# Dense projections of a hybrid encoder: three split float32r matmuls replaced by one float32 matmul

## The chip, the cores and the metric

One core of one Trainium2 chip runs the whole kernel. The metric is the device time of one execution in microseconds, the median of several runs.

## What is computed

A two-layer encoder trunk on 256 tokens of width 1024, all in float32. Layer 0 mixes tokens with a bidirectional diagonal state-space mixer, layer 1 with neighbourhood attention. Each is followed by a mixture of 32 experts (two of them for each token) and a gated embedding. The parts that matter here:

```python
def _rmsnorm(x, g):
    y = x * lax.rsqrt(jnp.mean(x * x, axis=-1, keepdims=True) + RMS_EPS)
    return y * g

for i in range(2):
    h = _rmsnorm(x, norm_mix[i])
    x = x + (_s5_mixer(h, ...) if i == 0 else _nat_mixer(h, nat_w_qkv[0], ...))   # qkv = h @ w_qkv, 1024 x 3072
    h = _rmsnorm(x, norm_ffn[i])
    x = x + _hier_moe(h, ...)
    gate = jax.nn.sigmoid(_rmsnorm(x, norm_ple[i]) @ ple_w_gate[i])               # 1024 x 1024
    x = x + gate * (p[i] @ ple_w_proj[i])
```

In the attention, q and k are normalised per head (64 values), and a score bias of relative positions is added.

## The kernel before

Every engine has its own program, written out by hand in order, with semaphores between them. The order in time is: state-space layer, MoE block 0, embedding gate 0 (`ple(0)`), qkv projection, attention with its output product, MoE block 1, embedding gate 1 (`ple(1)`), store.

**Weights.** SyncE's queue loads every weight in an order fixed in the program into a ring of six slots in SBUF. A slot's next load waits on the semaphore that says that its last content is used up; for the gate and qkv weights this is `split_done`. The gate weight of 1024 x 1024 comes as two halves of 512 columns (`ga`, `gb`), the qkv weight as six parts of 512 columns (0 and 1 are q, 2 and 3 are k, 4 and 5 are v), each 2 MB and each in one slot. `IT["ple"]` and `IT["qkv"]` hold their item numbers. A part has four chunks of two 128-row blocks; `place` numbers the chunks in the order in which TensorE takes them.

**Transposed x.** A norm's input x is kept in four pieces (128 tokens x 512 columns). For each, TensorE makes four transposes into a PSUM bank (`piece_T`, line 1714). For the dense products ScalarE copies the bank, rounded to float32r, into `hTh` (`piece_evict`, line 781), and VectorE then writes the remainder into `hTl` (`split_lo`, line 1141). The norm's per-token factor `rstd` is applied at the end, when the products are evicted; the norm's per-column gain goes into the weights.

**Weights' split.** For each 128-row block of 512 columns, ScalarE multiplies the loaded weights by the gain and rounds them to float32r into `dwh`, a ring of four chunks (`dense_hi`, line 814); VectorE writes the remainder in place of the loaded weights (`dense_lo`, line 1151). ScalarE waits for the DMA (`arrived`) and for `dwh` to come free.

**Product.** `dense_mm` (line 1741) makes, for each block and for each of the two token tiles, three float32r matmuls: high x by low weights, low x by high weights, high by high, all into one PSUM bank:

```python
for w, (a_, b_) in enumerate(((hTh, lo), (hTl, hi), (hTh, hi))):
    ins = mm(PS[:, b, :], a_[:, 2 * c + k, r], b_, ...)
```

**Order.** In `ple(i)` TensorE transposes four pieces of x, takes the four chunks of `ga`, three of `gb`, (for i = 0) the transposes of the first two pieces of the next norm, and the last chunk of `gb`. Those pieces are ready when `ple_gate` (ScalarE, sigmoid) and `ple_evict` (VectorE, product and sum) of the first columns are done. Then come qkv parts 0 and 1, interleaved by halves with the transposes of the last two pieces, and parts 2 to 5 in turn, into two pairs of PSUM banks. Each part is evicted by ScalarE (tokens 0 to 127) and VectorE (128 to 255) in `qkv_evict`; parts 0 to 3 go on through `square` (ScalarE), `sums` (VectorE), a power on GpSimd (`qk_pow`, line 728), `qk_norm` (VectorE), transposes on TensorE (`qk_T`, line 2146) and `q_evict` or `k_evict`. GpSimd issues the loads of the score bias (`bias_load`, line 743) in the same queue, one group before each power. TensorE's `qk_T` groups stand after chunk 2 of part 3, chunks 0 and 2 of part 4 and chunk 1 of part 5; the first block of `scores` stands after chunk 2 of part 5.

Elsewhere the kernel uses plain float32 matmuls on loaded weights: the state-space output product (line 1906), the experts (lines 1951 and 1977), the embedding projection (`proj`, line 2009) and the attention output product (line 2209).

Of the kernel before, what the change touches and what calls it, by code (L numbers as in the profile page):

```python
# [72 lines left out]
def program(nc, I, out):  # L73
    ctx = ExitStack()
    with ctx:
# [146 lines left out]
        for i in range(2):  # L222
            done.update({moe_item[i] + e: ("gu_done", NP * i + e // 2 + 1) for e in range(NE)})

            done.update({n: ("split_done", place[n if (n, 3) in place else IT["ple"][i][0], 3] + 1)
                         for n in IT["ple"][i]})
        done.update({n: ("split_done", place[n, 3] + 1) for n in IT["qkv"]})
# [31 lines left out]
        gain_of = {n: 2 for n in IT["ple"][0]}  # L259
        gain_of.update({n: 3 for n in IT["qkv"]})  # L260
        gain_of.update({n: 6 for n in IT["ple"][1]})

# [102 lines left out]
        hTh = at("hTh", [P, KD, T], F32R, A_XG)  # L365
        hTl = at("hTl", [P, KD, T], F32R, A_XG + 8192)
        dwh = at("dwh", [P, 4, 2, 512], F32R, A_XG + 16384)
        ringr = [at(f"ringr{s}", [P, KD, 512], F32R, A_R + s * RS * 4) for s in range(4)]
        SPLIT = {2: 0, 3: 1, 5: 2}

        def dense_w(n, c):

            s = items[n][0]
            return (ring[s][:, 1024 * c:1024 * c + 1024].rearrange("p (k n) -> p k n", k=2),
                    ringr[s][:, 2 * c:2 * c + 2, :])
# [61 lines left out]
        def _(sp):  # L437
# [105 lines left out]
            for i in range(2):  # L543
                if i:
                    for w, e in ((4, 0), (5, 1)):
                        sp.wait_ge(S("split_done"), place[IT["qkv"][w], 3] + 1)
                        load_gate(i, e)
                        load_up(i, e)
                        load_down(i, e)
# [212 lines left out]
        def _(ac):  # L762
# [14 lines left out]
            def piece_evict(n, m):  # L777
                c, t = divmod(m, 2)
                ac.wait_ge(S("x_T"), pieces(n) + m + 1)
                if n in SPLIT:  # L780
                    ac.activation(hTh[:, 4 * c:4 * c + 4, P * t:P * t + P],
                                  PS[:, 4 + 2 * t + c, :].rearrange("p (k t) -> p k t", k=4), ACT.Copy)\
                        .then_inc(S("hTh_ready"), 1)
                else:
                    ac.activation(hT[:, 4 * c:4 * c + 4, P * t:P * t + P],
                                  PS[:, 2 + t, :].rearrange("p (k t) -> p k t", k=4), ACT.Copy)\
                        .then_inc(S("hT_ready"), 1)
# [16 lines left out]

            def dense_hi(n, c):

                m = place[n, c]
                if c == 0:
                    arrived(ac, n)
                if m >= 4:  # L810
                    ac.wait_ge(S("split_done"), m - 3)
                for k in range(2):
                    g = 2 * c + k
                    ins = ac.activation(dwh[:, m % 4, k], dense_w(n, c)[0][:, k, :], ACT.Copy,  # L814
                                        scale=gcol[:, gain_of[n], g:g + 1])
                ins.then_inc(S("dense_hi"), 1)
# [145 lines left out]
            def moe(i):  # L962
# [24 lines left out]
                for c in range(4):  # L987
                    dense_hi(IT["ple"][i][0], c)
# [8 lines left out]
            def ple_gate(i, n):  # L997
                k = 4 * i + n
                c, t = divmod(n, 2)
                ac.wait_ge(S("split_done"), place[IT["ple"][i][2 * c], 3] + 1)  # L1000
# [6 lines left out]
            def ple(i):  # L1007
                n = 2 + 3 * i
                for m in range(4):
                    piece_evict(n, m)  # L1010
                for m in range(4):
                    piece_sq(n, m)
                gb = IT["ple"][i][2]
                for c in range(3):
                    dense_hi(gb, c)
                ple_gate(i, 0)
                ple_gate(i, 1)
                dense_hi(gb, 3)
                if i == 0:
                    q0, q1 = IT["qkv"][0:2]  # L1020
                    dense_hi(q0, 0)
                    dense_hi(q0, 1)
                    piece_evict(3, 0)
                    piece_evict(3, 1)
                    dense_hi(q1, 0)
                    piece_sq(3, 0)
                    piece_sq(3, 1)
                ple_gate(i, 2)
                ple_gate(i, 3)
                if i == 0:  # L1030
                    dense_hi(q1, 1)
                    dense_hi(q0, 2)
                    piece_evict(3, 2)
                    piece_evict(3, 3)
                    dense_hi(q0, 3)
                    piece_sq(3, 2)
                    piece_sq(3, 3)
                    dense_hi(q1, 2)
                    dense_hi(q1, 3)
# [5 lines left out]
            def qkv_evict(w):  # L1045
                ac.wait_ge(S("split_done"), place[IT["qkv"][w], 3] + 1)
# [23 lines left out]
            for w in range(2, 6):  # L1070
                for c in range(4):
                    dense_hi(IT["qkv"][w], c)
                    if (w, c) == (2, 1):
                        qkv_evict(0)
                        square(0)
                    if (w, c) == (4, 1):
                        q_evict(0)
                    if (w, c) == (4, 3):
                        q_evict(1)
                qkv_evict(w - 1)  # L1080
                if w < 5:
                    square(w - 1)
# [29 lines left out]
        def _(ve):  # L1112
# [24 lines left out]
            def split_lo(n, m):  # L1137
                c, t = divmod(m, 2)
                ve.wait_ge(S("hTh_ready"), 4 * SPLIT[n] + m + 1)
                r = hTh[:, 4 * c:4 * c + 4, P * t:P * t + P]  # L1140
                tt(hTl[:, 4 * c:4 * c + 4, P * t:P * t + P], PS[:, 4 + 2 * t + c, :].rearrange("p (k t) -> p k t", k=4),  # L1141
                   r.bitcast(F32), ALU.subtract).then_inc(S("hTl_ready"), 1)

            def dense_lo(n, c):

                m = place[n, c]
                ve.wait_ge(S("dense_hi"), m + 1)
                w, lo = dense_w(n, c)
                for k in range(2):
                    g = 2 * c + k  # L1150
                    ins = stt(lo[:, k, :], w[:, k, :], gcol[:, gain_of[n], g:g + 1], dwh[:, m % 4, k].bitcast(F32),  # L1151
                              ALU.mult, ALU.subtract)
                ins.then_inc(S("dense_lo"), 1)
# [401 lines left out]
            def ple(i):  # L1555
                ga, _, gb = IT["ple"][i]
                dense_lo(ga, 0)
                dense_lo(ga, 1)
                for m in range(4):
                    split_lo(2 + 3 * i, m)  # L1560
                dense_lo(ga, 2)
                dense_lo(ga, 3)
                stats(2 + 3 * i)
                for c in range(3):
                    dense_lo(gb, c)
                ple_evict(i, 0)
                ple_evict(i, 1)
                dense_lo(gb, 3)
                if i == 0:
                    q0, q1 = IT["qkv"][0:2]  # L1570
                    dense_lo(q0, 0)
                    dense_lo(q0, 1)
                    split_lo(3, 0)
                    split_lo(3, 1)
                    dense_lo(q1, 0)
                ple_evict(i, 2)
                ple_evict(i, 3)
                if i == 0:
                    dense_lo(q1, 1)
                    dense_lo(q0, 2)  # L1580
                    split_lo(3, 2)
                    split_lo(3, 3)
                    dense_lo(q0, 3)
                    stats(3)
                    dense_lo(q1, 2)
                    dense_lo(q1, 3)
# [5 lines left out]
            def qkv_evict(w):  # L1592
                ve.wait_ge(S("split_done"), place[IT["qkv"][w], 3] + 1)
# [25 lines left out]
            for w in range(2, 6):  # L1619
                for c in range(4):  # L1620
                    dense_lo(IT["qkv"][w], c)
                    if (w, c) == (2, 1):
                        qkv_evict(0)
                        sums(0)
                    if c == 1 and w > 2:
                        qk_norm(w - 2)
                    if (w, c) == (5, 1):
                        k_evict(2)
                if w == 2:
                    qk_norm(0)  # L1630
                qkv_evict(w - 1)
                if w < 5:
                    sums(w - 1)
# [54 lines left out]
        def _(pe):  # L1688
# [13 lines left out]
            def piece_T(n, m):  # L1702
# [3 lines left out]
                if n in SPLIT:  # L1706
# [25 lines left out]
            def dense_mm(n, c, b0, b1):  # L1732

                m = place[n, c]
# [367 lines left out]
            def ple(i):  # L2102
# [7 lines left out]
                for c in range(4):  # L2110
                    if c % 2 == 0:
                        pe.wait_ge(S("hTl_ready"), 4 * SPLIT[norm] + 2 + c)
# [13 lines left out]
            pe.wait_ge(S("hTl_ready"), 4 * SPLIT[3] + 2)  # L2126
# [6 lines left out]
            pe.wait_ge(S("hTl_ready"), 4 * SPLIT[3] + 4)  # L2133
# [131 lines left out]
```

## Time and profile before

| | |
|---|---|
| median of 3 runs | 796.95 us (794.77 to 798.34) |
| the profiled execution | 796.67 us, of which the span of its instructions is 794.9 us |
| TensorE matmul busy | 738.1 us, 93% of the span |
| VectorE, ScalarE, GpSimd busy | 409.2, 277.9, 111.2 us |
| granted TensorE clock, mean | 0.987 of full speed |
| DMA | 247.33 MB, mean 311 GB/s |

Busy time says how long an engine had an instruction under way, not that it was needed then; the chain that ended last says which work set the end. Matmuls overlap in the pipeline, so their mean duration is longer than their distance. The two dense stages lie at 384 to 478 us and at 766 to 789 us of the span.

### The profile page before, as it was taken

What the parts mean: (1) busy time and instruction counts of PE and PEld (TensorE: products, weight loads), DVE (VectorE), ACT (ScalarE), POOL (GpSimd) and SP (SyncE); (2) the same over time, 40 slices, a digit from 0 to 9 for tenths busy, and PEclk for the clock granted to TensorE, in tenths of its full rate; (3) what the DMA queues carried; (4) which work ended last, traced back from release to release, by engine and by line L of the source; (5) the groups of instructions that cost most, each with busy time, mean ns of one, the idle gap of its engine ahead of it and who ended that gap; (6) DMA issues with size and microseconds to landing.
All of it is one profiled execution on the core that took longest, in us unless ns stands there. A gap on an engine that the chain in (4) does not pass through costs nothing.

```text
span 794.9 us, 12786 instructions
## 1 busy us (share of the span) xinstructions
PE 738.1 (93%) x5121; PEld 470.4 (59%) x5121; DVE 409.2 (51%) x913; ACT 277.9 (35%) x521; POOL 111.2 (14%) x112
## 2 busy tenths in 40 slices
PE   4877789799999999989999998999999999999896
PEld 3755655465655555544788884555655555564465
DVE  6998833644343343432786868345443343434174
ACT  6351144252221222213675746425121222222163
POOL 5697320000000000000206621000000000000000
PEclk9989999999999999999999999999999999999999
DMA  8157693659999999999657789843999999999921
GB/s 274 42 142 222 172 356 127 264 206 423 420 421 420 420 421 421 421 420 397 220 206 236 215 265 327 337 196 113 421 421 420 421 421 421 421 419 421 406 95 53
DMA packets 64244, 247.33 MB, mean 311 GB/s; under 512 B 22244, under 2 KB 23832, under 8 KB 39224
## 3 DMA queue, kind: packets, MB, share of 16 engines
q1 hardware_dynamic: 62152, 243.14, 78.3%
q0 software_dynamic: 2032, 3.35, 1.9%
q8 instruction: 42, 0.69, 0.3%
q14 instruction: 18, 0.15, 0.1%
HBM read 242.85 MB, written 3.06 MB: 309 GB/s over the span
## 4 chain that ended last, share of the span: by engine, by line
PE 68%; DMA 10%; DVE 10%; SPq 5%; POOL 4%; issue 1%; ACT 1%; DVEq 0%
PE PS L1951 21%; PE PS L1741 14%; PE PS L1977 11%; DMA ring<-in_moe_w_down 6%; PE PS L1987 5%; PE PS L2209 4%; DMA ring<-in_moe_w_up 3%; PE PS L1906 3%; POOL s5V L680 2%; PE PS L1921 2%; PE PS L2009 2%; POOL s5W L680 2%; SPq L471 2%; SPq L455 1%; PE PS L1839 1%
## 5 line engine op out<-in xcount | busy, mean ns | idle before, releaser
L1951 PE MATMUL PS<-ring,xw 128*64 128x256 f32 x2016 | 227.7, 379 | 6.8 <-DMA ring<-in_moe_w_up 3.0
L1951 PEld LDWEIGHTS PS<-ring,xw 128*64 128x64 f32 x2016 | 149.5, 137 | 88.8 <-issue 17.5
L1977 PE MATMUL PS<-ring,actT 128*64 128x512 f32 x512 | 116.9, 598 | 2.4 <-DMA ring<-in_moe_w_down 1.3
L1442 DVE COPY actT<-PS 128x256 f32<-128x256 f32 x32 | 13.6, 424 | 159.7 <-PE PS L1960 159.7
L959 ACT ACTIVATE ohi<-PS 128x512 fp32r<-128x512 f32 x64 | 38.2, 597 | 145.8 <-PE PS L1977 145.8
L1456 DVE TENSOR_TENSOR olo<-PS,ohi 128x512 fp32r<-128x512 f32 x64 | 44.3, 692 | 83.3 <-ACT ohi L959 83.2
L652 POOL TENSOR_TENSOR rstd<-ms,mhalf 128x2 f32<-128x2 f32 x6 | 4.2, 706 | 589.8 <-DVE ms L1126 583.4
L1977 PEld LDWEIGHTS PS<-ring,actT 128*64 128x64 f32 x512 | 34.3, 136 | 67.9 <-issue 66.2
L951 ACT ACTIVATE act<-PS,wslot 128x256 f32<-128x256 f32 x32 | 15.2, 476 | 164.9 <-PE PS L1951 164.9
L1425 DVE SCALAR_TENSOR_TENSOR act<-rows,pid 128x256 f32<-128x256 f32 x128 | 61.9, 483 | 14.0 <-DMA rows<-rows_d 10.6
L1741 PE MATMUL PS<-ringr,hTh 128*128 128x512 f32 x160 | 63.2, 395 | 1.4 <-DVE hTl L1141 1.4
L1741 PE MATMUL PS<-dwh,hTh 128*128 128x512 f32 x160 | 62.4, 390 | 0.0
L1741 PE MATMUL PS<-dwh,hTl 128*128 128x512 f32 x160 | 62.3, 389 | 0.0
L1151 DVE SCALAR_TENSOR_TENSOR ringr<-ring,gcol,dwh 128x512 fp32r<-128x512 f32 x80 | 55.3, 746 | 12.0 <-ACT dwh L814 12.0
L814 ACT ACTIVATE dwh<-ring,gcol 128x512 fp32r<-128x512 f32 x80 | 52.2, 714 | 15.7 <-PE PS L1741 13.3
L1987 PE MATMUL PS<-ohi,selT 128*128 128x512 f32 x128 | 53.9, 421 | 0.2
L1987 PE MATMUL PS<-olo,selT 128*128 128x512 f32 x128 | 50.4, 394 | 0.0
L945 ACT ACTIVATE xw<-xg 128x512 f32 x60 | 38.1, 636 | 3.1 <-issue 2.4
L1741 PEld LDWEIGHTS PS<-ringr,hTh 128*128 128x128 f32 x160 | 30.0, 188 | 8.0 <-DVE hTl L1141 1.9
L1741 PEld LDWEIGHTS PS<-dwh,hTh 128*128 128x128 f32 x160 | 30.0, 188 | 6.4
L1741 PEld LDWEIGHTS PS<-dwh,hTl 128*128 128x128 f32 x160 | 30.1, 188 | 5.9
L2209 PE MATMUL PS<-ring,oT 128*128 128x512 f32 x64 | 30.1, 605 | 0.0
(326 smaller groups left out, 960.4 us busy)
## 6 DMA issues: line engine op xcount, KB each, us to landing
ring<-in_moe_w_down SPq DMA_DIRECT2D x64, 1024.0 KB, 20.8
ring<-in_moe_w_up SPq DMA_DIRECT2D x64, 1024.0 KB, 18.8
ring<-in_moe_w_gate SPq DMA_DIRECT2D x62, 1024.0 KB, 16.5
ring<-in_nat_w_qkv SPq DMA_DIRECT2D x6, 2048.0 KB
ring<-in_ple_w_gate SPq DMA_DIRECT2D x4, 2048.0 KB
ring<-in_s_w_out SPq DMA_DIRECT2D x2, 2048.0 KB
ring<-in_nat_w_o SPq DMA_DIRECT2D x2, 2048.0 KB
ring<-in_s_w_in SPq DMA_DIRECT2D x1, 2048.0 KB
```

Source lines behind the costliest of these rows:

```text
L680: pool.tensor_tensor(dst, dst, tmp[n % 2][:, :, :, :], ALU.subtract if minus else ALU.add)\
L814: ins = ac.activation(dwh[:, m % 4, k], dense_w(n, c)[0][:, k, :], ACT.Copy, scale=gcol[:, gain_of[n], g:g + 1])
L945: ac.activation(xw[:, p % 2, :, CAP * h_:CAP * h_ + CAP], xg[:, :, bass.ds(f, CAP)], ACT.Copy)\
L959: ac.activation(ohi[:, 512 * n:512 * n + 512], PS[:, 2 + n, :], ACT.Copy)\
L1151: ins = stt(lo[:, k, :], w[:, k, :], gcol[:, gain_of[n], g:g + 1], dwh[:, m % 4, k].bitcast(F32), ALU.mult, ALU.subtract)
L1425: link(stt(act[:, p % 2].rearrange("p k f -> p (k f)"), slotrow[:, n % 2, :], pid[:, p:p + 1], row, ALU.is_equal, ALU.mult, accum_out=wpar ...
L1456: tt(olo[:, cs], PS[:, 2 + n, :], ohi[:, cs].bitcast(F32), ALU.subtract)\
L1741: ins = mm(PS[:, b, :], a_[:, 2 * c + k, r], b_, start=(c, k, w) == (0, 0, 0), stop=(c, k, w) == (3, 1, 2))
L1951: ins = mm(PS[CAP * h_:CAP * h_ + CAP, 0, FF * u:FF * u + FF], xw[:, p % 2, k, CAP * h_:CAP * h_ + CAP], wv[h_][:, FF * k:FF * k + FF], st ...
L1977: ins = mm(PS[CAP * h_:CAP * h_ + CAP, 2 + n, :], actT[:, k, CAP * h_:CAP * h_ + CAP], wd[h_][:, k, 512 * n:512 * n + 512], start=k == 0, ...
L1987: ins = mm(PS[:, 4 + 2 * t + n, :], selT[p % 2][:, P * t:P * t + P], o_half[:, 512 * n:512 * n + 512], start=(p, w) == (0, 0), stop=(p, w) ...
L2209: ins = mm(PS[:, 4 + 2 * c + t, :], oT[:, k, P * t:P * t + P], wv[:, k, :], start=k == 0, stop=k == KD - 1)
```

## The change

The products of gates and qkv become one float32 matmul for each block and token tile, directly on the loaded weights. The gain is multiplied into the transposed x as VectorE evicts it from PSUM (`hT_gain`, into `hTg`, float32). `dense_hi`, `dense_lo`, `split_lo`, `dwh` and ScalarE's part of `piece_evict` for these norms go. TensorE waits for each part's DMA itself. The semaphore `split_done` is now `dense_done`. The order of TensorE's work stays; in the qkv part, the loops of ScalarE and VectorE are written anew without the splits.

```diff
-                if n in SPLIT:
-                    ac.activation(hTh[:, 4 * c:4 * c + 4, P * t:P * t + P],
-                                  PS[:, 4 + 2 * t + c, :].rearrange("p (k t) -> p k t", k=4), ACT.Copy)\
-                        .then_inc(S("hTh_ready"), 1)
...
-            def dense_hi(n, c):
...
-                    ins = ac.activation(dwh[:, m % 4, k], dense_w(n, c)[0][:, k, :], ACT.Copy,
-                                        scale=gcol[:, gain_of[n], g:g + 1])
...
@@ ScalarE, qkv
-            for w in range(2, 6):
-                for c in range(4):
-                    dense_hi(IT["qkv"][w], c)
...
+            for w in range(5):
+                qkv_evict(w)
+                if w < 4:
+                    square(w)
+                if w in (2, 3):
+                    q_evict(w - 2)
@@ VectorE
-            def split_lo(n, m):
+            def hT_gain(n, m):
+
                 c, t = divmod(m, 2)
...
+                ve.wait_ge(S("x_T"), pieces(n) + m + 1)
+                tt(hTg[:, 4 * c:4 * c + 4, P * t:P * t + P], PS[:, 4 + 2 * t + c, :].rearrange("p (k t) -> p k t", k=4),
+                   bc(gcol[:, BLOCK_GAIN[n], 4 * c:4 * c + 4], 2, P), ALU.mult).then_inc(S("hTg_ready"), 1)
...
-                    ins = stt(lo[:, k, :], w[:, k, :], gcol[:, gain_of[n], g:g + 1], dwh[:, m % 4, k].bitcast(F32),
-                              ALU.mult, ALU.subtract)
...
@@ VectorE, qkv
+            for w in range(4):
+                qkv_evict(w)
+                if w:
+                    qk_norm(w - 1)
+                sums(w)
+            k_evict(2)
+            qk_norm(3)
+            qkv_evict(4)
             k_evict(3)
@@ TensorE, dense_mm
-                m = place[n, c]
-                pe.wait_ge(S("dense_lo"), m + 1)
+                if c == 0:
+                    arrived(pe, n)
                 for k in range(2):
                     for t, b in enumerate((b0, b1)):
-                        r = slice(P * t, P * t + P)
-                        hi, lo = dwh[:, m % 4, k, :], dense_w(n, c)[1][:, k, :]
-                        for w, (a_, b_) in enumerate(((hTh, lo), (hTl, hi), (hTh, hi))):
-                            ins = mm(PS[:, b, :], a_[:, 2 * c + k, r], b_, start=(c, k, w) == (0, 0, 0),
-                                     stop=(c, k, w) == (3, 1, 2))
-                ins.then_inc(S("split_done"), 1)
+                        ins = mm(PS[:, b, :], hTg[:, 2 * c + k, P * t:P * t + P], dense_w(n, c)[:, k, :],
+                                 start=(c, k) == (0, 0), stop=(c, k) == (3, 1))
+                ins.then_inc(S("dense_done"), 1)
```

## Rows read from the trace of the kernel before

**Rows 1.** The page, part 2: tenths of busy or granted clock, and GB/s.

```profile
PEclk9989999999999999999999999999999999999999
GB/s 274 42 142 222 172 356 127 264 206 423 420 421 420 420 421 421 421 420 397 220 206 236 215 265 327 337 196 113 421 421 420 421 421 421 421 419 421 406 95 53
```

**Rows 2.** The chain that ended last, in order of time: start us, us, what.

```profile
113.50 10.30 PE PS L1906 x24
...
382.83 1.30 DVE hTl L1141 x2
384.17 19.34 PE PS L1741 x84
403.51 0.88 PE PS L1714 x8
...
413.44 35.41 PE PS L1741 x156
...
455.18 0.87 PE PS L2146 x8
...
517.27 3.44 PE PS L2209 x8
...
766.56 22.09 PE PS L1741 x96
```

**Rows 3.** Groups by line and shape: count, busy us, mean ns, idle before.

```profile
L1741 PE MATMUL PS<-ringr,hTh 128*128 128x512 f32 x160 | 63.2, 395 | 1.4 <-DVE hTl L1141 1.4
...
L1151 DVE SCALAR_TENSOR_TENSOR ringr<-ring,gcol,dwh 128x512 fp32r<-128x512 f32 x80 | 55.3, 746 | 12.0 <-ACT dwh L814 12.0
...
L814 ACT ACTIVATE dwh<-ring,gcol 128x512 fp32r<-128x512 f32 x80 | 52.2, 714 | 15.7 <-PE PS L1741 13.3 <-DMA ring<-in_ple_w_gate 2.2
...
L1247 DVE TENSOR_TENSOR s5T<-PS,mask 128x512 f32<-128x512 f32 x8 | 5.4, 681 | 2.6 <-POOL s5V L680 2.4
```

**Rows 4.** Timelines of ScalarE, TensorE and VectorE before the first dense stage.

```profile
374.52 5.01 ACT L814 ACTIVATE dwh<-ring,gcol 128x512 fp32r<-128x512 f32 x8 [1.06 <-DMA ring<-in_ple_w_gate]
...
381.56 1.91 PE L1714 MATMUL PS<-ident,x 128*128 128x128 f32 x16
...
382.20 2.06 ACT L781 ACTIVATE hTh<-PS 128x512 fp32r<-128x512 f32 x4 [2.67 <-PE PS L1714]
...
382.83 2.48 DVE L1141 TENSOR_TENSOR hTl<-PS,hTh 128x512 fp32r<-128x512 f32 x4 [0.29 <-ACT hTh L781]
```

**Rows 5.** ScalarE's timeline in gate 0, where the first half's products end.

```profile
394.02 1.28 ACT L1004 ACT_TABLE_LOAD   x1
395.38 1.27 ACT L1004 ACTIVATE sg<-PS,rstd 128x512 f32<-128x512 f32 x2
```

**Rows 6.** GpSimd's timeline during qkv: bias loads and one power.

```profile
419.96 4.79 POOL L743 DMA_DIRECT2D bias<-bias_d  x8
...
452.45 4.81 POOL L743 DMA_DIRECT2D bias<-bias_d  x8
460.14 3.35 POOL L728 TENSOR_TENSOR qrs<-qms,mhalf 128x16 f32<-128x16 f32 x1 [2.88 <-DVE qms L1604]
```

**Rows 7.** VectorE's timeline during qkv: one reduction and one multiplication.

```profile
458.63 1.22 DVE L1603 TENSOR_REDUCE qss<-sq 128x16 f32<-128x1024 f32 x1 [1.57 <-ACT sq L1059]
...
463.52 1.22 DVE L1609 TENSOR_TENSOR qk<-qk,qrs 128x1024 f32<-128x1024 f32 x1 [0.82 <-POOL qrs L728]
```

**Rows 8.** SyncE's timeline, DMA issues (us to landing), and windows (the last number is GB/s).

```profile
395.37 0.40 SPq L449 DMA_DIRECT2D ring<-in_nat_w_qkv  x1
...
bias<-bias_d POOLq DMA_DIRECT2D x4, 72.0 KB, 6.8
...
390.00:392.00 2.00, 2.00 (x10) 1.66 (x9) 0.75 (x3) 1.28 (x2) 2.00 (x4) 1.00 0.24 14
...
404.00:406.00 2.00, 2.00 (x12) 1.71 (x11) 1.29 (x2) 2.00 (x4) 0.00 (x0) 1.00 0.00 0
...
762.00:764.00 2.00, 2.00 (x6) 0.76 (x5) 2.00 (x4) 0.00 (x0) 0.00 (x0) 1.00 0.00 0
```

More of the change, by code:

```diff
@@ L223, in program @@
             done.update({moe_item[i] + e: ("gu_done", NP * i + e // 2 + 1) for e in range(NE)})
-            done.update({n: ("split_done", place[n if (n, 3) in place else IT["ple"][i][0], 3] + 1)
+            done.update({n: ("dense_done", place[n if (n, 3) in place else IT["ple"][i][0], 3] + 1)
                          for n in IT["ple"][i]})
-        done.update({n: ("split_done", place[n, 3] + 1) for n in IT["qkv"]})
+        done.update({n: ("dense_done", place[n, 3] + 1) for n in IT["qkv"]})
         done.update({n: ("wo_done", 2 * c + 2) for c, n in enumerate(IT["wo"])})
@@ L258, in program @@
         ROW_GAIN = {1: 1, 4: 5}
-        gain_of = {n: 2 for n in IT["ple"][0]}
-        gain_of.update({n: 3 for n in IT["qkv"]})
-        gain_of.update({n: 6 for n in IT["ple"][1]})
         def pieces(n):
@@ L363, in program @@
         rr = at("rr", [P, 4, 2 * TT], F32, A_W + 1184)
[L365 to L369, printed above, removed]
+        hTg = at("hTg", [P, KD, T], F32, A_XG)
+        DENSE = {2: 0, 3: 1, 5: 2}
         def dense_w(n, c):
             s = items[n][0]
-            return (ring[s][:, 1024 * c:1024 * c + 1024].rearrange("p (k n) -> p k n", k=2),
-                    ringr[s][:, 2 * c:2 * c + 2, :])
+            return ring[s][:, 1024 * c:1024 * c + 1024].rearrange("p (k n) -> p k n", k=2)
         pT = at("pT", [P, 2, T], F32, A_H + 8192)
@@ L545, in _ @@
                     for w, e in ((4, 0), (5, 1)):
-                        sp.wait_ge(S("split_done"), place[IT["qkv"][w], 3] + 1)
+                        sp.wait_ge(S("dense_done"), place[IT["qkv"][w], 3] + 1)
                         load_gate(i, e)
@@ L779, in piece_evict @@
                 ac.wait_ge(S("x_T"), pieces(n) + m + 1)
-                if n in SPLIT:
-                    ac.activation(hTh[:, 4 * c:4 * c + 4, P * t:P * t + P],
-                                  PS[:, 4 + 2 * t + c, :].rearrange("p (k t) -> p k t", k=4), ACT.Copy)\
-                        .then_inc(S("hTh_ready"), 1)
[L784 to L787, printed above, removed]
+                ac.activation(hT[:, 4 * c:4 * c + 4, P * t:P * t + P],
+                              PS[:, 2 + t, :].rearrange("p (k t) -> p k t", k=4), ACT.Copy)\
+                    .then_inc(S("hT_ready"), 1)
             def piece_hi(n, m):
@@ L803, in front @@
                     piece_hi(n, m)
-            def dense_hi(n, c):
-                m = place[n, c]
[L808 to L813, printed above, removed]
-                    ins = ac.activation(dwh[:, m % 4, k], dense_w(n, c)[0][:, k, :], ACT.Copy,
-                                        scale=gcol[:, gain_of[n], g:g + 1])
-                ins.then_inc(S("dense_hi"), 1)
             def norm_evict(dst, t):
@@ L986, in moe @@
                 out_hi(i, NP - 1)
-                for c in range(4):
-                    dense_hi(IT["ple"][i][0], c)
                 def more(n):
@@ L999, in ple_gate @@
                 c, t = divmod(n, 2)
-                ac.wait_ge(S("split_done"), place[IT["ple"][i][2 * c], 3] + 1)
+                ac.wait_ge(S("dense_done"), place[IT["ple"][i][2 * c], 3] + 1)
                 ac.wait_ge(S("rstd_ready"), 3 + 3 * i)
@@ L1009, in ple @@
                 for m in range(4):
-                    piece_evict(n, m)
-                for m in range(4):
                     piece_sq(n, m)
-                gb = IT["ple"][i][2]
-                for c in range(3):
-                    dense_hi(gb, c)
                 ple_gate(i, 0)
                 ple_gate(i, 1)
-                dense_hi(gb, 3)
                 if i == 0:
[L1020 to L1025, printed above, removed]
                     piece_sq(3, 0)
@@ L1030, in ple @@
                 if i == 0:
[L1031 to L1035, printed above, removed]
                     piece_sq(3, 2)
                     piece_sq(3, 3)
-                    dense_hi(q1, 2)
-                    dense_hi(q1, 3)
             moe(0)
@@ L1045, in qkv_evict @@
             def qkv_evict(w):
-                ac.wait_ge(S("split_done"), place[IT["qkv"][w], 3] + 1)
+                ac.wait_ge(S("dense_done"), place[IT["qkv"][w], 3] + 1)
                 if w == 0:
@@ L1069, in _ @@
             link(ac.activation(qkw8[:, :], qkw[:, 0:1], ACT.Copy, scale=1 / math.sqrt(HD)))
-            for w in range(2, 6):
-                for c in range(4):
-                    dense_hi(IT["qkv"][w], c)
[L1073 to L1082, printed above, removed]
+            for w in range(5):
[4 more added lines that the diff above has]
+                    q_evict(w - 2)
             ac.activation(warm[:, :], ones[:, 0:1], ACT.Exp)
@@ L1135, in piece_lo @@
                    hhi[:, t, :, 64 * c:64 * c + 64].bitcast(F32), ALU.subtract).then_inc(S("hlo_ready"), 1)
-            def split_lo(n, m):
+            def hT_gain(n, m):
                 c, t = divmod(m, 2)
[L1139 to L1150, printed above, removed]
-                    ins = stt(lo[:, k, :], w[:, k, :], gcol[:, gain_of[n], g:g + 1], dwh[:, m % 4, k].bitcast(F32),
-                              ALU.mult, ALU.subtract)
-                ins.then_inc(S("dense_lo"), 1)
+                ve.wait_ge(S("x_T"), pieces(n) + m + 1)
+                tt(hTg[:, 4 * c:4 * c + 4, P * t:P * t + P], PS[:, 4 + 2 * t + c, :].rearrange("p (k t) -> p k t", k=4),
+                   bc(gcol[:, BLOCK_GAIN[n], 4 * c:4 * c + 4], 2, P), ALU.mult).then_inc(S("hTg_ready"), 1)
             ve.wait_ge(S("lam_loaded"), 48)
@@ L1555, in ple @@
             def ple(i):
-                ga, _, gb = IT["ple"][i]
-                dense_lo(ga, 0)
-                dense_lo(ga, 1)
                 for m in range(4):
-                    split_lo(2 + 3 * i, m)
-                dense_lo(ga, 2)
-                dense_lo(ga, 3)
+                    hT_gain(2 + 3 * i, m)
                 stats(2 + 3 * i)
-                for c in range(3):
-                    dense_lo(gb, c)
                 ple_evict(i, 0)
                 ple_evict(i, 1)
-                dense_lo(gb, 3)
                 if i == 0:
[L1570 to L1575, printed above, removed]
+                    hT_gain(3, 0)
+                    hT_gain(3, 1)
                 ple_evict(i, 2)
@@ L1578, in ple @@
                 if i == 0:
[L1579 to L1583, printed above, removed]
+                    hT_gain(3, 2)
+                    hT_gain(3, 3)
                     stats(3)
-                    dense_lo(q1, 2)
-                    dense_lo(q1, 3)
             moe(0)
@@ L1592, in qkv_evict @@
             def qkv_evict(w):
-                ve.wait_ge(S("split_done"), place[IT["qkv"][w], 3] + 1)
+                ve.wait_ge(S("dense_done"), place[IT["qkv"][w], 3] + 1)
                 if w == 0:
@@ L1618, in _ @@
             ve.wait_ge(S("qkw_loaded"), 64)
[L1619 to L1633, printed above, removed]
+            for w in range(4):
[6 more added lines that the diff above has]
+            qkv_evict(4)
             k_evict(3)
@@ L1705, in piece_T @@
                 pe.wait_ge(S("x_piece"), pieces(n) + m + 1)
-                if n in SPLIT:
+                if n in DENSE:
                     b = 4 + 2 * t + c
@@ L2111, in ple @@
                     if c % 2 == 0:
-                        pe.wait_ge(S("hTl_ready"), 4 * SPLIT[norm] + 2 + c)
+                        pe.wait_ge(S("hTg_ready"), 4 * DENSE[norm] + 2 + c)
                     dense_mm(ga, c, 4, 6)
@@ L2125, in _ @@
             q0, q1 = IT["qkv"][0:2]
-            pe.wait_ge(S("hTl_ready"), 4 * SPLIT[3] + 2)
+            pe.wait_ge(S("hTg_ready"), 4 * DENSE[3] + 2)
             dense_mm(q0, 0, 0, 1)
@@ L2132, in _ @@
             dense_mm(q1, 1, 2, 3)
-            pe.wait_ge(S("hTl_ready"), 4 * SPLIT[3] + 4)
+            pe.wait_ge(S("hTg_ready"), 4 * DENSE[3] + 4)
             dense_mm(q0, 2, 0, 1)
```

1 line of the change is left out of this document (removed).

## The prediction

> **What bounds the kernel now.** I read the chain that ended last first, in order of time, then the instruction groups, then the timelines of each engine around the two dense stages, and last the DMA windows. The kernel has four regimes: the state-space layer, two MoE blocks, and between and behind them the projections that the change rewrites. The MoE blocks run with the load queue full: the GB/s row holds 420 in slices 10 to 18 and 29 to 38 [rows 1], and the change touches nothing in them. In the dense stages the load queue is far from full (206 to 265 GB/s in slices 20 to 24), and the chain is TensorE alone: the split matmuls of line 1741, broken only by transposes and by one score block [rows 2]. So work taken from TensorE there counts in full, and work taken from VectorE and ScalarE counts only where it stands on the chain.
>
> There are 160 products of one 128-row block of weights with one token tile, each made of three float32r matmuls; the group row has 160 of the first kind, and the other two kinds have as many, 480 in all [rows 3]. A group's mean duration (395 ns) overlaps its neighbours, so I take the pace from the chain: 19.34 us for 84, 35.41 for 156, 22.09 for 96, that is 0.230, 0.227 and 0.230 us each [rows 2]. The first dense stage holds 384 of them (eight pieces of the chain, 87.8 us in all), the second 96 (22.1 us). Together 109.9 us.
>
> **The change, part by part.**
>
> *Plain float32 matmuls.* 480 go, 160 come: 128 in the first stage (16 for each of two gate halves and six qkv parts), 32 in the second. Their shape, 128 x 128 stationary and 128 x 512 float32 moving from the ring, is in this kernel already: 24 in 10.30 us on line 1906 and 8 in 3.44 us on line 2209 [rows 2], 0.429 and 0.430 us each, back to back, with a new stationary tile each. At 0.430 the first stage needs 55.0 us, the second 13.8. Gain: 87.8 - 55.0 = 32.8 and 22.1 - 13.8 = 8.3, together 41.1 us. The bounds of this term are narrow: 0.427 to 0.435 us give 160 x 0.003 = 0.5 more or 0.8 less.
>
> The Trainium skill, "FP8 and Floating Point Precision", section "TensorE Precision Notes", says the opposite of these rows: true float32 takes four passes through the array, and only the reduced form one. By this rule the change would lose time. The rows have the float32 matmul at 1.9 times the float32r one, not four, so the sum goes by them and the rule is a rival below.
>
> *The splits of weights.* 80 ScalarE copies of 714 ns and 80 VectorE operations of 746 ns go [rows 3]. None is on the chain of the first stage; they ran beside TensorE, so they count nothing by themselves. What they hid: TensorE now waits for the weights' own loads. In the first stage the first half's weights were being read at 374.52 [rows 4], nine microseconds before use, and by 390 the DMA had fallen to 14 GB/s [rows 8]: both gate halves and the first two qkv parts had landed by then, and at the new pace they are wanted at 383.5, 390.4, 398.1 and 402.4. A later part was issued at 395.37 and traffic was zero at 404 [rows 8]: under 9 us from issue to landing. At the new pace part 2 is issued when the first gate half is done (390.4) and wanted at 412.9, part 3 issued 398.1, wanted 419.8, parts 4 and 5 issued 409.4 and 412.9, wanted 427.5 and 436.1. The least distance between issue and want is 18 us, twice a load's nine. In the second stage traffic is zero at 762 [rows 8], and the second half is wanted at about 772.8. So I cost the loads at nothing.
>
> *Norm's scale put into transposed x.* ScalarE's rounding copy and VectorE's subtraction, one after the other, become one VectorE multiplication for each piece. Its price is not shown; the nearest is a PSUM by broadcast multiply of the same 128 x 512, 681 ns [rows 3], and I take 0.69. Were the broadcast inside the row to double it, 0.7 us would be added to the start of each stage; that end stays in the range. Now: transposes from 381.56 over 1.91 us, ScalarE at 382.20, VectorE from 382.83 at 0.62 a piece, TensorE at 384.17 after two pieces [rows 2, 4]. After: VectorE starts at 382.2, two pieces are done by about 383.5, when the transposes end too. Gain 0.65 us, in both stages: 1.3 us.
>
> *Sigmoid and the next norm.* ScalarE's table load (394.02, 1.28 us [rows 5]) stood behind a split and just fitted in; without splits ScalarE is idle from about 382 and loads it early. With gate half 0 done at 390.4, two sigmoids of 0.7 and four VectorE steps of 0.69 put the first two pieces of x ready at 392.8 and 394.2; TensorE wants to transpose them after three quarters of the second half, at 395.5: 1.3 us to spare. The other two pieces: half 1 done 398.1, ready 400.6 and 402.0; TensorE comes at 401.6 and at 402.0. I count 0.4 us of stall here.
>
> *The q and k norm.* This is what runs late next, and it is the only narrow place. VectorE's mean squares go to GpSimd, which takes 3.35 us for the power and stands, in its own queue, behind bias loads of 4.8 us (the first and the last of four; the two between issue four DMAs, not eight, so half of that) [rows 6]; VectorE's reduction and multiplication are 1.22 us each [rows 7]. Followed step by step at the new pace: GpSimd issues the first bias loads until about 412, takes the powers at 412.8, 418.8 and 424.9, issues the last bias loads 428.3 to 433.1, takes the last power until 436.5, and VectorE multiplies until 437.7. TensorE wants the last transposes of k at 439.5. Slack 1.8 us. The loads of the bias must land before VectorE's first score at 442.7; 6.8 us from issue [rows 8] makes 439.9. Behind the reordered VectorE queue stand the eviction of v's first half and k's last eviction, 438.4 and 442.0; the scores that need them come at 442.1 and 444.4. All hidden, by little.
>
> *What follows.* With its six groups of transposes (5.2 us) and the first score block (0.6) the stage ends, with the second scores, 33.1 us earlier than now. Attention, its output product, the router and the second MoE block are released by TensorE's own progress and shift as a whole; the prefetch of the first experts starts at the last two qkv parts, keeping its distance to the MoE block. The tail behind the last dense matmul (788.65 to 794.9: sigmoid, product, sum, store) stays as it is.
>
> Sum: 41.1 + 1.3 - 0.4 = 42.0 us. The profiled execution took 796.67 us (span 794.9, 1.8 around it), 0.3 under the median 796.95. So 796.67 - 42.0 = 754.7, and for a median 755.
>
> **Rivals.**
>
> *Four passes.* If a float32 matmul of these operands took four times a pass of 0.228 us, 160 x 0.912 = 145.9 us would stand against 109.9: 36 us more, less 1.3 at the starts: 831 us, slower than before. It decides from 0.69 us a matmul on. Against it: three lines of the kernel at 0.43, of the same shape, in full stream. 2%. By the skill's figure of four passes at 2.4 GHz (an estimate from "FP8 and Floating Point Precision", 0.853 us) it would be about 822; no row here shows such a matmul.
>
> *GpSimd's chain becomes the bound.* If its bias issues or powers slip, each microsecond beyond 1.8 goes to TensorE. One or two issue blocks of 4.8 us too many, less the slack of 1.8, give 3.0 to 7.8 us: 758 to 763. For it: 3.35 us powers in strict order behind DMA issues. Against it: the steps are from rows and still leave slack. 13%.
>
> *The loads are the bound.* With the stage a third shorter the same bytes (six parts, two output parts and the first experts) need a higher rate. If weights arrived only at the 220 GB/s that the stage shows now, eight loads of 2.1 MB would take 76 us instead of 62: 14 us lost, 769. Against it: the stage is at 390 to 410 GB/s whenever a load is under way, and zero between; the 220 is demand. 4%.
>
> *The gain is lost in MoE's load-bound stretch.* If the second MoE block started short of experts, it would end by its loads, and the first stage's 33 us could shrink to 20 (768). Against it: prefetch and MoE start shift together. 2%.
>
> *TensorE's clock.* The PEclk row is at 9 or more in all slices but one [rows 1], and the stage leaves no new gap in TensorE's work; left out as a case of its own.
>
> **How the numbers follow.** Likeliest, 79%: all terms as costed, 755 us, own range 752.5 to 757.5 (matmul pace, multiply price, stalls of 0 to 2 us, a median that wanders by 0.2 to 0.3%). GpSimd's chain 13% (758 to 763), loads 4%, MoE 2%, four passes 2%. The range for 8 in 10, drawn towards the GpSimd case's middle: 752 to 760. A measurement of this kernel can tell about 0.5%, 4 us. All cases but four passes are faster by far more: faster 0.97, same 0.01, slower 0.02.
>
> **What the profile after should show.** 160 matmuls on the dense line at 0.43 us pace, in place of 480; the first stage some 61 us long instead of 94; ScalarE busy about 58 us less (52.2 of the splits, three groups of copies of 2.06) and VectorE about 55 us less; a first dense matmul about 1.3 us after ScalarE used to start copying; PE idle in the stage under 1 us, and where any, before the transposes of x's last pieces or of k's last ones, released by VectorE; granted clock 1.00; DMA above 300 GB/s there; MoE's length unchanged to 0.5 us. The prediction is wrong if the matmul's pace differs from 0.43, if waits on the ring's loads or on k's norm appear on the chain, or if the second MoE block grows.

## The result: 825 us, slower, and where the profile after puts it

The changed kernel takes 825.22 us (median of 4 runs, 822.82 to 826.92) against 797.13 us before: ratio 1.0354, 95% interval 1.0317 to 1.0391. The forecast was 755 us. In the experiments below, two runs fell into a slower state of the chip (835.54 us of kernel half, 1330.24 us of kernel cols) and are left out of the medians. The profiled execution has a span of 824.3 us, 29.4 more than before.

The page of the changed kernel, part 1, and its costliest group of the dense products (line 1649 is the new `dense_mm`):

```profile
PE 765.6 (93%) x4961; PEld 440.4 (53%) x4961; DVE 355.6 (43%) x833; ACT 222.0 (27%) x429; POOL 109.2 (13%) x112
...
L1649 PE MATMUL PS<-ring,hTg 128*128 128x512 f32 x320 | 139.1, 593 | 0.1
...
L2117 PE MATMUL PS<-ring,oT 128*128 128x512 f32 x64 | 30.1, 605 | 0.0
```

VectorE has 53.6 us less to do and ScalarE 55.9 us less, as forecast, and none of it shows in the time. TensorE has 27.5 us more. The count of matmuls says why: the code makes 160 products (four chunks of two blocks for two token tiles in each of ten parts), and the trace has 320 matmuls. One float32 product is two matmul records (entries of the trace), each with its own weight load. The last row says the same of a line that the change left alone: the attention output product is called 2 x 2 x 8 = 32 times and has 64 records, in this trace as in that of before.

The chain that ended last in the changed kernel, in order of time (start us, us, what):

```profile
384.21 1.30 DVE hTg L1087 x2
385.56 24.30 PE PS L1649 x56
409.86 0.87 PE PS L1625 x8
410.73 10.30 PE PS L1649 x24
...
421.90 44.64 PE PS L1649 x104
466.54 0.87 PE PS L2054 x8
...
498.11 3.63 PE PS L1649 x8
...
788.92 1.30 DVE hTg L1087 x2
790.27 27.75 PE PS L1649 x64
```

A record takes 0.429 us (44.64 for 104), as I had read in [rows 2]; a product, being two, takes 0.859. The three float32r matmuls that it replaces took 3 x 0.2285 = 0.685 (0.227 to 0.230 each in the chain of before). The chain is the same as in [rows 2], still TensorE alone, and its sum explains the time:

| term | before | after | difference |
|---|---|---|---|
| dense products, first stage (eight pieces of the chain each) | 87.8 | 110.4 | +22.6 |
| dense products, second stage | 22.1 | 27.8 | +5.7 |
| from the last projection matmul to the first product, two stages | 2 x 2.45 | 2 x 1.82 | -1.3 |
| start of the second half of the first projection, ahead of all changed code | 378.29 | 380.30 | +2.0 |

Together 29.0 of the 29.4 us. The last term is no work of the change: the same point lies anywhere from 377.40 (v3one) to 381.74 (two_qkw) in the profiled executions below, so the first MoE block's end spreads by 4 us. Without it the terms make 27.0 us, and the medians differ by 28.1.

### The profile page after: what moved, and what is told of

The parts are those of the page before. It is cut to its first block, busy times and chain, and to the rows that moved or that the text cites. A ratio compares the mean times of both kernels' runs of the same rounds, so it can differ in the third digit from the quotient of the medians.

```text
span 824.3 us, 12281 instructions
## 1 busy us (share of the span) xinstructions
PE 765.6 (93%) x4961; PEld 440.4 (53%) x4961; DVE 355.6 (43%) x833; ACT 222.0 (27%) x429; POOL 109.2 (13%) x112
## 4 chain that ended last, share of the span: by engine, by line
PE 69%; DVE 10%; SPq 8%; DMA 6%; POOL 4%; issue 1%; ACT 1%; DVEq 0%
PE PS L1859 21%; PE PS L1649 17%; PE PS L1885 10%; DMA ring<-in_moe_w_down 6%; PE PS L1895 5%; PE PS L2117 4%; PE PS L1814 3%; SPq L463 2%; POOL s5V L672 2%; SPq L456 2%; SPq L441 2%; PE PS L1829 2%; SPq L447 2%; PE PS L1917 2%; POOL s5W L672 2%
## 5 line engine op out<-in xcount | busy, mean ns | idle before, releaser
L1649 PE MATMUL PS<-ring,hTg 128*128 128x512 f32 x320 | 139.1, 593 | 0.1
L1649 PEld LDWEIGHTS PS<-ring,hTg 128*128 128x128 f32 x320 | 60.1, 190 | 73.0 <-issue 72.4
L1814 PE MATMUL PS<-ring,yT 128*128 128x512 f32 x64 | 28.4, 593 | 0.0
L1895 PEld LDWEIGHTS PS<-ohi,selT 128*128 128x128 f32 x128 | 24.1, 188 | 5.7 <-DVE olo L1391 1.1
L1895 PEld LDWEIGHTS PS<-olo,selT 128*128 128x128 f32 x128 | 24.1, 189 | 4.6 <-issue 0.5
L1486 DVE TENSOR_TENSOR sg<-sg,PS 128x512 f32<-128x512 f32 x8 | 5.5, 684 | 41.0 <-ACT sg L976 41.0
L1657 PE MATMUL PS<-iota_slot,ident 128*128 128x512 f32 x40 | 21.4, 674 | 0.0
L1774 PE MATMUL PS<-s5V,s5W 64*128 64x128 f32 x256 | 16.2, 277 | 5.1 <-issue 2.2
```

The costliest lines, as they stand in the source:

```text
L1649: ins = mm(PS[:, b, :], hTg[:, 2 * c + k, P * t:P * t + P], dense_w(n, c)[:, k, :], start=(c, k) == (0, 0), stop=(c, k) == (3, 1))
L1657: mm(PS[:, b, :], ident[:, :], iota_slot[:, :], start=True, stop=True)
L1814: ins = mm(PS[:, 4 + 2 * (n % 2) + w, :], yT[4][:, k, P * t:P * t + P], wv[:, k, 512 * c:512 * c + 512], start=k == 0, stop=k == 3)
L1895: ins = mm(PS[:, 4 + 2 * t + n, :], selT[p % 2][:, P * t:P * t + P], o_half[:, 512 * n:512 * n + 512], start=(p, w) == (0, 0), stop=(p, w) ...
```

## Experiments

### The pace that was forecast, with half of each product

```diff
-                for k in range(2):
+                for k in range(1):
```

> The changed kernel with half of each dense product: of the two 128-row blocks of a chunk only the first is multiplied, so the other half of the contraction is left out. 80 float32 products instead of 160; everything else as in the changed kernel. Theory A (a float32 product is two instruction pairs on TensorE, 0.859 us together, and this alone made the kernel slower): 80 x 0.859 = 68.7 us less than the changed kernel's 825.2, so 756.5, within 2 us. This is the TensorE time per chunk (1.72 us) that the prediction had assumed, so it also tests the prediction's other terms. Rival B (the q and k norm with GpSimd's queue, or the weights' loads, would have bound the stage anyway): 759 to 769, with TensorE idle before the transposes of k or before a part. Rival C (the loss is from waits, not from the length of the products): above 790.

Measured: 756.62 us (median of three runs), ratio 0.9471 (0.9426 to 0.9516) against 798.87 us before in the same job. That is theory A's 756.5, and below rival B's 759. The group of line 1649 and the first stage's end in the chain:

```profile
L1649 PE MATMUL PS<-ring,hTg 128*128 128x512 f32 x160 | 70.5, 594 | 0.1
```

```profile
436.18 5.15 PE PS L1649 x12
441.33 0.89 PE PS L2054 x8
...
444.08 10.46 DMA vb<-vt
454.54 0.14 issue
454.68 0.69 PE PS L2099 x16
```

And GpSimd's timeline, bias loads and the last power:

```profile
428.86 4.81 POOL L735 DMA_DIRECT2D bias<-bias_d  x8
433.68 2.93 POOL L720 TENSOR_TENSOR qrs<-qms,mhalf 128x16 f32<-128x16 f32 x1
```

This kernel gives TensorE the length of product that I had assumed for the whole change. It is 42.3 us under before, where I had said 42.0. The stage starts at 385.19, 1.7 us later than I had worked out, by the spread named above. Apart from that, the last bias loads end at 433.7 (forecast 433.1), the last power at 436.6 (436.5), and TensorE comes to the last transposes of k at 441.3 (439.5 + 1.7 = 441.2). Up to there the schedule was right; only the length of a product was not. What I had not seen is the load of v's bands: the four loads of the first bands were issued 442.5 to 444.6, and the larger two took 8.7 us to land, where the same loads take 2.4 in the changed kernel and 4.0 in the one before. The loads of the first two experts were under way beside them (issued from 437.9 and from 446.5 on). The first products of probabilities and values waited 1.1 us for the bands. Nor had I seen what follows the wait, which I had ruled out as a case of its own: the granted clock is 1.00 up to 455 us, with TensorE busy only 0.66 of the 2 us from 452 to 454, then 0.66 from 455 to 456 and 0.50, the lower of its two levels (1.2 of 2.4 GHz), from 456 to 458. The same groups of the chain, first there and then behind it:

```profile
455.36 1.06 PE PS L2075 x16
456.42 1.04 PE PS L2087 x4
...
460.55 0.60 PE PS L2075 x16
461.15 0.59 PE PS L2087 x4
```

With the products of values (1.05 against 0.62) and the first output products (2.03 against 1.91) this is 1.5 us lost. The profiled execution shows it: its span is 37.8 us shorter than before, which is, within 0.1, the 42.0 less the 1.7 us of the later start, the wait of 1.1 and these 1.5. That the medians agree to 0.3 us is partly luck.

### Columns or instructions

```diff
-                        ins = mm(PS[:, b, :], hTg[...], dense_w(n, c)[:, k, :], ...)
+                        for q in (0, 1):
+                            s_ = slice(256 * q, 256 * q + 256)
+                            ins = mm(PS[:, b, s_], hTg[...], dense_w(n, c)[:, k, s_], ...)
```

> The changed kernel with each float32 product of 512 columns issued as two of 256 columns on the same stationary tile: twice the matmuls and weight loads, the same columns streamed. Theory A (the pace is set by streamed columns, 0.43 us for 512 columns in each of two instruction pairs): 640 records of 0.215 us, no change, 825 to 828. Rival D (the pace is set per instruction pair, by the weight load and issue): the 137 us of dense products grow, up to twice as long (962) if nothing depends on the columns.

Measured: 825.83 us (median of three runs), 1.0331 (1.0281 to 1.0381) of before, the changed kernel's time. The groups by shape of this kernel:

```profile
L1651 PE MATMUL PS<-ring,hTg 128*128 128x256 f32 x640 | 139.9, 380 | 0.1
L1651 PEld LDWEIGHTS PS<-ring,hTg 128*128 128x128 f32 x640 | 120.9, 190 | 16.9 <-DVE hTg L1087 0.6 <-issue 0.2
```

320 more weight loads, and the busy time goes from 139.1 to 139.9 us. The columns streamed set the pace, and a record costs what its columns cost, 0.216 us for 256 (44.90 us for 208 in its chain); the weight loads of 190 ns are hidden behind even the halved matmuls. Rival D falls.

### One of the three float32r products less

```diff
-                        for w, (a_, b_) in enumerate(((hTh, lo), (hTl, hi), (hTh, hi))):
+                        for w, (a_, b_) in enumerate(((hTh, lo), (hTh, hi))):
```

> The kernel before with two of the three float32r products: low x by high weights is left out, all splits stay. 320 instead of 480 float32r matmuls at 0.2285 us. Theory A (the dense stages are bound by TensorE's products alone): 36.5 us less than before, 797.1 - 36.5 = 760.6, within 2 us. Rival B (other engines or loads are just behind): the splits of VectorE need 1.42 us a chunk against 1.83 us of products, so only waits on norm, bias or loads could hold it up: 765 to 775.

Measured: 781.23 us, 0.9789 (0.9752 to 0.9826). It is faster than before, by 1.7 to 2.5%, but misses the forecast by 20 us. The chain of this kernel:

```profile
404.73 2.65 DVE ringr L1151 x4
407.38 1.20 DVE hTl L1141 x2
408.58 1.32 DVE ringr L1151 x2
410.26 1.16 POOL rstd L652
411.42 1.58 POOL qkw L719 x3
413.00 5.77 DMA qkw<-in_nat_k_norm
...
420.47 1.19 DVE ringr L1151 x2
```

TensorE's products are off the chain from 389.5 to 463.1 us. VectorE with its splits is on it, and a 1 KB load of the norm's gains, issued late in GpSimd's queue, on which ScalarE waits 7.6 us. In the kernel before, the same wait was 1.36 us and hidden. Theory A as I had put it (the stages are bound by products alone) doesn't hold at this length of product. To see that this was no odd execution, I ran the same kernel once more.

> The two-product kernel of run two once more, for one look: whether the 20 us by which it missed its forecast stand in the same places. Theory E (with less TensorE work, the 7.6 us wait of ScalarE on the load of the q and k norm's gains, and the coupled chain of VectorE's splits, mean squares and GpSimd's power, take over): span 777 to 781, the same wait on that load of about 7 us. Theory F (a single disturbed execution): span near 760.

Measured: 784.11 us in a single run, ScalarE waiting 7.5 us at the same place. The span is 782.4, 1.4 above theory E's range, and the start of the second half of the first projection lies 3.9 us later than in run two (381.74 against 377.82). Theory E stands in the main, F falls.

### The scale in x alone

```diff
+                tt(hTf[...], PS[:, 4 + 2 * t + c, :]..., bc(gcol[:, BLOCK_GAIN[n], 4 * c:4 * c + 4], 2, P), ALU.mult)
...
-                    ins = ac.activation(dwh[:, m % 4, k], w[:, k, :], ACT.Copy, scale=gcol[...])
+                    ins = ac.activation(dwh[:, m % 4, k], w[:, k, :], ACT.Copy)
```

> One part of the change alone: the norm's scale is multiplied into transposed x by VectorE (a pass of its own, then ScalarE's rounding copy and VectorE's subtraction), the weights are split without the scale, and the three float32r products stay. Theory A: products unchanged, only the start of each dense stage is later, by four multiplications of 0.62 us less the 0.6 us copy's wait that they replace, about 1.9 us at each of two stages: 797.1 + 3.8 = 801. Rival (moving the scale is itself what costs): over 805.

Measured: 802.89 us, 1.0055 (1.0034 to 1.0075), or 4 us over the 798.87 of before, and within 2 us of the forecast. The chain at the start of its first stage:

```profile
379.51 2.48 DVE x L1529 x4
381.99 2.41 DVE ringr L1159 x4
384.40 2.39 DVE hTf L1142 x4
386.79 1.21 DVE hTl L1149 x2
388.01 0.04 issue
388.05 4.15 PE PS L1754 x17
```

From VectorE's first sum to the first product are 8.5 us, against 6.8 before (377.41 to 384.17): 1.8 us at this stage. So moving the scale costs 4 us when the split stays. When the split goes it costs nothing: the changed kernel starts its products 1.82 us after the projection, against 2.45. It does not explain the 28.

### Rounded weights, two products and one

The failed forecast of the two-product kernel named its own waits. These kernels take them away: weights rounded in place, half by each engine, and the gains' load moved forward.

```diff
-                for k in range(2):      # ScalarE: high part of both blocks into dwh
-                    ins = ac.activation(dwh[:, m % 4, k], ...)
+                ac.activation(r[:, 0, :], w[:, 0, :], ACT.Copy, scale=gcol[...])
...
-                    ins = stt(lo[:, k, :], w[:, k, :], gcol[...], dwh[...], ALU.mult, ALU.subtract)
+                ts(r[:, 1, :], w[:, 1, :], gcol[...], None, ALU.mult)
...
-            pool.wait_ge(S("x_piece"), pieces(4))
+            pool.wait_ge(S("x_piece"), pieces(2) + 4)
```

> The kernel before with two float32r products, and the splits of the weights cut to one rounding in place: ScalarE rounds the even and VectorE the odd 128-row block of a chunk (0.7 us each, in place of 1.34 and 1.42 us), high x and low x are both multiplied by the rounded weights, and the weights' low part is left out. The load of the q and k norm's gains is issued right after the first gate's x is ready. Theory E (TensorE's length of product binds once the splits and that load are out of its way): 797.1 - 36.5 = 760.6, with up to 2 us for the loads of v's bands: 760 to 763. Rival (another wait takes the place of those): 770 to 780.

> As v2 with one float32r product: x is rounded too, so the low parts of both factors are left out. TensorE's dense work falls by 73 us against before. Theory A alone would give 797.1 - 73.1 = 724. Theory E says that other engines bind here: for each qkv part VectorE has 4 roundings of 0.75, an eviction of 0.75, a reduction and a multiplication of 1.22 each, 6.4 us in all, and a part's load takes 5.4 us, both against 3.7 us of products: 735 to 748, with waits on the norm's chain and on loads.

Measured: two products 766.77 us, 0.9589 (0.9564 to 0.9615); one product 758.11 us, 0.9492 (0.9471 to 0.9513). Both missed their forecasts: v2 by 4 us, v1 by 10. v2 gains 14 us over the kernel with full splits, from the same number of products; how much of this is the rounding and how much the moved load was not separated. In v1, TensorE's own dense work is 73 us shorter than before and the kernel only 41. Part of the chain of v1:

```profile
425.95 3.09 POOL qrs L727
429.07 0.86 DVE qk L1602
429.92 0.59 ACT qk L1046
430.51 1.35 issue
431.86 1.07 ACT sq L1054
432.95 1.23 DVE qss L1596
434.20 0.18 DVE qms L1597
434.39 0.07 issue
434.46 3.10 POOL qrs L727
```

This is the norm's chain, once round for a part in 8.5 us (425.95 to 434.46): my rival B, at last the bound. The same round stands in v2's chain (powers start at 425.17, 433.66 and 442.17), and behind it the load of v's bands with 9.13 us, where that kernel misses its forecast. In v1 TensorE also lost clock:

```profile
383.00:440.00 57.00, 40.18 (x174) 29.71 (x172) 36.63 (x66) 40.65 (x72) 34.46 (x40) 0.91 0.97 296
440.00:460.00 20.00, 16.74 (x176) 10.21 (x176) 16.73 (x28) 10.77 (x45) 4.13 (x8) 0.83 1.03 352
```

These are two windows of v1; the first number after the length is TensorE's busy time, the third from the end the granted clock. TensorE had been busy 40.18 of the first 57 us. Within them the clock is 1.00 from 410 to 415 us, where TensorE is busy 1.89 of 5, then 0.62 to 420 and 0.50 to 425; it is 1.00 from 430 to 440, where TensorE is busy 6.11 of 10, and 0.50 from 441 to 443. Four float32r matmuls at 440.67 took 2.04 us, and four of the same line at 407.83, at a clock of 1.00, 1.09: about half as long.

### The order of the changed kernel on top

```diff
-            for w in range(2, 6):
-                for c in range(4):
-                    dense_lo(IT["qkv"][w], c)
...
+            for w in range(4):
+                qkv_evict(w)
+                if w:
+                    qk_norm(w - 1)
+                sums(w)
+                if w < 3:
+                    for c in range(4):
+                        dense_lo(IT["qkv"][w + 3], c)
```

> v2 with the order of the changed kernel in the qkv stage: ScalarE and VectorE evict a part and start its norm first and then round the part three ahead, as far as its weights have landed. Two float32r products on rounded weights, the weights' low part left out. Theory E: TensorE's waits inside the qkv stage of v2, about 2.5 us over 64.3 us of its own work, go: 763 to 765. Rival (the order does not matter, what is left is the load of v's bands, which queues behind the experts' loads, and the spread of the first MoE block): no change against v2, 766 to 768.

> v3 with one float32r product on rounded x, the low parts of both factors left out. Theory E: in v1 the chain of eviction, square, reduction, GpSimd's power and multiplication came round once for each part, 8.5 us; with the roundings out of its way it should come down to the 6 to 7 us of GpSimd's own queue (3.1 us power, 2.3 or 4.8 us of bias loads): 4 to 8 us less than v1, 750 to 754. Rival: no change, 757 to 759.

Measured: v3 764.27 us, 0.9576 (0.9554 to 0.9597), inside its forecast; v3one 755.88 us, 0.9469 (0.9443 to 0.9494), outside. Neither interval is apart from that of v2 or v1, so the order alone is not shown to matter. The chain of v3 says what it met instead:

```profile
405.17 10.94 PE PS L1731 x48
416.12 17.04 DMA ring<-in_nat_w_qkv
433.17 0.03 issue
433.19 1.34 DVE ringr L1143 x4
```

The load of a qkv part, which I had taken at 9 us from [rows 8], took 17 here, and the rounding waited for it. It was not alone: the part before it had been issued 3.6 us earlier, the output weights followed 7.3 us later, and bias loads ran beside them. The DMA engines were busy throughout (share 1.05 from 416 to 433 us), at 310 GB/s. Theory E in its form for v3one (GpSimd's queue sets the pace, 750 to 754) isn't borne out, nor is its rival (757 to 759): in its chain the same kind of load stands for 21.8 us.

All of v1, v2, v3 and v3one beat the kernels before and after. They aren't the same computation: v2 and v3 leave out the low part of the weights, v1 and v3one that of x too.

## Why the prediction was wrong

**The step that failed** is the first term: "Their shape, 128 x 128 stationary and 128 x 512 float32 moving from the ring, is in this kernel already: 24 in 10.30 us on line 1906 and 8 in 3.44 us on line 2209 [rows 2], 0.429 and 0.430 us each". The pace was read rightly, and what it was the pace of was not. 24 and 8 are records, and a plain float32 product leaves two. I multiplied the pace of a record by 160 products from the code. The counts of other plain float32 matmul lines would have shown the mistake: line 1977 of the kernel before has 512 records for 2 x 16 x 2 x 2 x 2 = 256 calls. On the other side I had counted rightly, 480 records for 480 float32r matmuls, and so compared a half with a whole. The term was -41.1 us; measured it is +28.3 us (22.6 + 5.7), and the correct sum from my own rows, 320 x 0.4295 - 109.9 = +27.5, less 1.3, would have given 823.

**The rival that I gave 2%** was the right one. I argued against it with three lines at 0.43. They were no evidence against four passes, being half products, and "no row here shows such a matmul" was wrong: those very rows did. The Trainium skill's rule ("FP8 and Floating Point Precision", "TensorE Precision Notes": true float32 takes four passes through the array) agrees with the trace: 0.859 us a product against 0.2285 for a float32r matmul is 3.8 times, and its four passes at 2.4 GHz (853 ns, an estimate from that page) are the 859 ns within 1%. The estimate of 822 that stood beside the rival hit within 0.4%. Where rows and a stated rule differ by a clean factor of two, the count under the rows should have been checked first.

**Most other steps held.** The start of each stage came 0.63 us earlier (forecast 0.65); the scale's multiplication takes 681 ns a piece (0.69). Splits of 55 us an engine were hidden and gave nothing. The stall of 0.4 us at x's last pieces isn't on the chain of the half-product kernel either, nor of the changed one. The weights' loads, the norm's chain and the bias loads stayed hidden at the forecast pace (half), and all the more at the real one. MoE and the clock didn't move in the changed kernel: the PEclk in the dense windows is 1.00 before and after. At the forecast pace (half) the clock did move behind the wait for v's bands, which cost 1.5 us; the prediction had put that term at nothing. The profile signs that I named were right as tests: the pace per product differs from 0.43, and nothing else does.

**Rival B and the loads** were sized for the wrong place. At the forecast pace they cost nothing but 1.1 us of v's bands and the clock behind it. They bind at 7.3 us of products a part, together with the splits (two) and still with one rounding (v2), and at 3.7 us a part with one rounding (v1).

## What to carry to other kernels

Before a pace from one line is used for another, divide its records by the calls in the code: in these traces a plain float32 matmul is two records, a float32r matmul and a transpose one. Where TensorE is the bound and other engines have slack, a split into three float32r products (0.685 us for 128 x 512) is faster than one float32 product (0.859), although it has three times as many matmuls in the code and work for two more engines. And when products get shorter, look for what has been waiting unseen: here a 1 KB load at the end of a queue went from a hidden 1.36 us to 7.6 us on the chain.

## What the runs showed of the hardware that I had not expected

- A float32 product of 512 columns streams in 0.859 us, in two matmuls of 0.429; in pieces of 256 columns the total is the same, with twice the weight loads (139.1 and 139.9 us busy).
- Where TensorE stood idle for part of the time, its granted clock fell to the lower level and came back: in v1 from 1.00 to 0.50 at 420 to 425 us, behind 5 us in which it was busy 1.89, and again to 0.50 at 441 to 443; in half to 0.50 at 456 to 458. In the dense stages of the kernels before and after it stays 1.00. In v1's chain the last two groups of products and their score blocks stand for 6.2 us, some 3 us more than at the full clock (an estimate from 0.2285 us a matmul, and 0.60 and 0.64 us a score block in the chain of before).
- A 2 MB load that took under 9 us alone in the kernel before took 17.0 us in v3, in a stretch that it shared with other weights and small bias loads; the 192 KB loads of v's first bands took 8.7 us in half, beside experts' loads, and 2.4 in the changed kernel, where traffic fell to 8 GB/s by 498 us; those of the second bands took 8.2 there, again beside experts' loads. What each stream takes from the others was not measured.
